# First stage of a two-layer latent/context kernel: one k-tile of modulation per pair of loads, and four products split in two parts

## The chip, the core and the metric

The kernel runs on one core of a Trainium2 chip. The metric is the device time of one execution in microseconds (us). Shorter is better. TensorE (PE) does the matmuls, VectorE (DVE), ScalarE (ACT) and GpSimd (POOL) the elementwise work. Data come by DMA: the queue of SyncE (SP, "q1" in the DMA views), that of ScalarE ("q10") and that of GpSimd ("q0"). All of them share the core's 16 DMA engines.

## The reference

Two layers work on 256 latent tokens of width 2048, and a context of 256 tokens is used by the first. Only the start of layer 0 is touched by the change:

```python
mod_lat = silu(c) @ ada_w[0] + ada_b[0]          # 2048 -> 6 * 2048: shift, scale, gate, ...
mod_ctx = silu(c_ctx) @ ada_w[0] + ada_b[0]
h_lat = rms_norm(x, g) * (1 + sc1) + sh1          # 256 x 2048
h_ctx = rms_norm(ctx, g) * (1 + csc1) + csh1      # 256 x 2048
qkv_lat, kv_ctx = h_lat @ w_qkv, h_ctx @ w_qkv[:, 2048:]
```

After it come attention, a dense MLP, the Fourier mixing layer, a second MLP and a norm. Everything is float32. A product of float32 matrices is made of three matmuls of a high and a low part: hi by hi, hi by lo, lo by hi.

## The kernel before

**Layout.** A k-tile is 128 of the 2048 input features. The tokens are turned so that features lie on the partitions (`xT`, then `h_hi` and `h_lo`, all in tile `hh`). The projection is done in groups of k-tiles: group 0 is k-tiles 0 and 1, group 1 is 2 and 3, then groups of four. Product `r` accumulates one block of 128 tokens by 512 output columns over the k-tiles of its group in one PSUM bank. Products 0 to 3 take w_qkv columns 0 to 1023 for the latent tokens. Each k-tile of these columns is one slice of the weights: slice 0 is k-tile 0, slice 1 is k-tile 1, each 128 x 1024. Two slices make one load of 1 MB.

**Weights.** SP loads `raw` (three buffers of 1 MB, `load_first` for loads 0 to 5, line 568). ACT copies a slice to its high part (`split_hi(s)`, line 727) and DVE subtracts to get the low part (`split_lo(s)`, line 1201). Before load 0 SP waits until modulation piece 1 has landed; then it issues raw load 0, raw load 1, the context (`c_rows`, 2 MB, line 594) and raw load 2 without another wait. Raw load 3 waits for slices 0 and 1 to be split, raw load 4 for slices 2 and 3, raw load 5 for slices 4 and 5.

**Modulation.** POOL loads `ada_w` in pieces of 1 MB (`load_start(n)`, line 652). Pieces 0 to 3 fill four `spare` buffers and are issued at once. Piece 4 waits for the context rows to land; pieces 4, 5, 6 are then issued together, and piece 7 waits for PE to have used piece 4, and so on. Pieces 0 to 7 (`first_v`) have rows of 256 columns, 1 KB, in DRAM: pieces 0 and 1 are the shift of k-tiles 0 and 1 (first and second half of the inputs), pieces 2 and 3 the scale of the same k-tiles. Pieces 4 to 7 do the same for k-tiles 2 and 3. Pieces from 8 on have rows of 512 columns, 2 KB.

PE multiplies a piece with `silu` (`first_piece(n)`, line 1887), into bank 6. When four pieces are in, ACT copies the rows out (`rows_out(0)`, line 777), PE turns them into columns (`first_cols(0)`, line 1896), and DVE adds the bias and makes the gain (`take_first`, lines 1318 and 1321). ACT then scales and shifts k-tiles 0 and 1 (`shape(0, 0)`, lines 789 and 793), and DVE makes the low part (`lower(0, 0)`, line 1351). Only then can product 0 start (lines 1848 to 1850).

**Order on each engine** is written out by hand. An engine does its instructions strictly in that order, waits included:

```python
# PE:  piece 0, piece 1, bias turns, piece 2, turn_input 0, 1, piece 3, turn_input 2, first_cols(0), turn_input 3, 4, 5,
#      product 0, 1, turn_input 6, 7, product 2, 3, ..., 8, piece 4, product 9, context turns, piece 5, product 10, ..., piece 6, ...
# ACT: x_out 0, 1, rows_out(0), split_hi(0), shape(0, 0), split_hi(1), x_out 2 to 5, split_hi(2), x_out 6, 7,
#      first_copy 0, 1, split_hi(3), first_copy 3, split_hi(4), split_hi(5), squares and norm of the context, ...
# DVE: take_first(0, 0), split_lo(0), lower(0, 0), split_lo(1), take_first(0, 1), split_lo(2), copy, split_lo(3), ...
```

`turn_input(i)` turns k-tiles 2i and 2i+1 of the normalised input into a PSUM bank (line 2116), and `x_out(i)` copies them to `xT` (line 769). Banks 0 to 3 hold turns 0 to 3 and are then the banks of products 0 to 3. The context rows are squared (line 755), normalised (line 1309) and turned (line 2146) later.

Of the kernel before, what the change touches and what calls it, by code (L numbers as in the profile page):

```python
# [136 lines left out]
def start_slot(n):  # L137

    return 3 + n if n < 4 else (n - 4) % 3


def vector_slot(i):

    if i < 8:
        return (7, 3)[i % 2]
    if 16 <= i < 48:
        return early_slot(i - 16)
    return i % 2
# [32 lines left out]

def start_count(n):

    return sum(start_slot(m) == start_slot(n) for m in range(n + 1))


def vector_count(i):

    return sum(start_slot(m) == vector_slot(i) for m in range(32)) + sum(vector_slot(m) == vector_slot(i) for m in range(i + 1))


def summed_before(i):
# [52 lines left out]
def layer_block(nc, x, c, ctx_in, c_ctx, ada_w, ada_b, norm_mix_g, norm_mlp_g, w_qkv, q_g, k_g, w_o,  # L245
# [118 lines left out]
    def sem(name):  # L364
        return stack.enter_context(nc.semaphore(name))
# [3 lines left out]
    c_in = sem("c_in")  # L369
    small_in = sem("small_in")  # L370
    x_in = sem("x_in")
    ctx_rows_in = sem("ctx_rows_in")
    rope_in_sem = sem("rope_in_sem")
    dft_in_sem = sem("dft_in_sem")
# [110 lines left out]
    wf_v = fourier_w[0].rearrange("(q k p) (b n) -> b q p k n", p=P, k=4, n=512)  # L485
    wqkv_first = w_qkv[0].rearrange("(g k p) (i n) -> g i p k n", p=P, k=2, n=NC)
    start_v = ada_w[0].rearrange("(q k p) (m g c) -> g m q p k c", p=P, k=4, g=4, c=512)
    first_v = ada_w[0].rearrange("(q k p) (m g c) -> g m q p k c", p=P, k=8, g=8, c=256)

    w1_v = [w1[l].rearrange("(q k p) (b n) -> b q p k n", p=P, k=4, n=512) for l in range(2)]  # L490

# [58 lines left out]
    def _(sp):  # L550
# [33 lines left out]
                                 gate_rows[v != 0][32 * j:32 * j + 32, :]).then_inc(gate_in, 16)  # L584

        sp.dma_start(ident[:, :], ident_in).then_inc(c_in, 16)
        sp.wait_ge(ada_in[start_slot(1)], 16)
        for p in range(24):
            if p < 6:
                load_first(p)  # L590
            else:
                load_columns(p, wqkv_v[p // 6, column_block(p)])
            if p == 1:
                sp.dma_start(c_rows[:, :, :], ctx_in[0].rearrange("(a p) d -> p a d", p=P)).then_inc(ctx_rows_in, 16)
            if p == 14:
                sp.wait_ge(prod_done, 48)
                sp.dma_start(rope[:, :, :, :], rope_in.rearrange("a (t p) d -> p a t d", p=P)).then_inc(rope_in_sem, 16)
                sp.dma_start(gains[:, 0, :], q_g[0].partition_broadcast(P)).then_inc(rope_in_sem, 16)
                sp.dma_start(gains[:, 1, :], k_g[0].partition_broadcast(P)).then_inc(rope_in_sem, 16)
# [41 lines left out]
    def _(pool):  # L641
        def load_start(n):

            if n >= 7:
                pool.wait_ge(ada_mm, n - 2)
            if n == 4:
                pool.wait_ge(ctx_rows_in, 16)
            if n < 8:
                dst, src = ring(start_slot(n)).rearrange("p (k c) -> p k c", k=8), first_v[n // 4, n % 4 // 2, n % 2]
            else:  # L650
                dst, src = ring(start_slot(n)).rearrange("p (k c) -> p k c", k=4), start_v[n // 8, n % 8 // 4, n % 4]
            pool.dma_start(dst, src).then_inc(ada_in[start_slot(n)], 16)

        def load_vector(i):

# [55 lines left out]
    def _(act):  # L711
# [60 lines left out]
        def rows_out(c):  # L772
# [60 lines left out]
        def heads_out(i, bank):  # L833
# [7 lines left out]
                dst = qT[:, 4 * b:4 * b + 4, tt * P:(tt + 1) * P]  # L841
            act.activation(dst, src, ACT.Copy).then_inc(head_T_out, 1)

        x_out(0)
        x_out(1)
        rows_out(0)
        split_hi(0)
        shape(0, 0)
        split_hi(1)
        x_out(2)  # L850
        x_out(3)
        x_out(4)
        x_out(5)
        split_hi(2)
# [341 lines left out]
    def _(dve):  # L1196
# [115 lines left out]
        def take_first(c, n):  # L1312

            dst, kts = (mod_col, modc_col)[n], group_tiles(c)
            dve.wait_ge(col_mm, c + 1)
            dve.wait_ge(vec_ready, 3)
            cols = ps[:, 6, 0:8].rearrange("p (m t v) -> p v m t", m=2, v=2)
            nc.vector.tensor_tensor(dst[:, 0:32].rearrange("p (m k) -> p m k", m=2)[:, :, kts], cols[:, n],
                                    bias_col[:, 0:32].rearrange("p (m k) -> p m k", m=2)[:, :, kts], ALU.add).then_inc(start_mods, 1)
            dve.wait_ge(start_mods, 2 * c + n + 1)  # L1320
            nc.vector.scalar_tensor_tensor(a_col[:, n, kts], dst[:, 16 + kts.start:16 + kts.stop], 1.0,
                                           misc[:, V_MIX + kts.start:V_MIX + kts.stop], ALU.add, ALU.mult).then_inc(a_ready, 1)

        def copy_first(r):

# [20 lines left out]
        def lower(c, n):  # L1346

            src, hi, lo = ((xT, h_hi, h_lo), (ctxT, hc_hi, hc_lo))[n]
            kts = group_tiles(c)
            dve.wait_ge(hhi_ready, 2 * c + n + 1)  # L1350
            nc.vector.tensor_tensor(lo[:, kts, :], src[:, kts, :], hi[:, kts, :].bitcast(F32),  # L1351
                                    ALU.subtract).then_inc(h_ready, 1)

        def add_product(r):

# [71 lines left out]
        for i, (dst, w) in enumerate(((bias_col[:, 0:96], 96), (bias_col[:, 96:192], 96), (misc[:, 32:96], 64))):  # L1427
            dve.wait_ge(vec_T, 3)
            nc.vector.tensor_copy(dst, ps[:, 7, i * P:i * P + w]).then_inc(vec_ready, 1)
        take_first(0, 0)  # L1430
        split_lo(0)
        lower(0, 0)
        split_lo(1)
        take_first(0, 1)
        split_lo(2)
        copy_first(2)
# [406 lines left out]
    def _(pe):  # L1843
# [8 lines left out]
        def tile_out(bank0, j):  # L1852
            return ps[:, bank0 + j // 2, (j % 2) * T:(j % 2 + 1) * T]

        def product(r):

            p, cb, tt = product_at(r)
            c = r // 16
            if r < 5:
                pe.wait_ge(x_T_out, (1, 2, 3, 4, 7)[r])  # L1860
            elif r == 33:
                pe.wait_ge(ctx_T_out, 7)
            else:
                pe.wait_ge(*flushed(bank_before(r)))
            hi, lo = (h_hi, h_lo) if tt < 2 else (hc_hi, hc_lo)
            pe.wait_ge(h_ready, 2 * c + 1 + tt // 2)
            tok = slice((tt % 2) * P, (tt % 2 + 1) * P)
            kts = group_tiles(c)
            n = kts.stop - kts.start
            for k in range(n):  # L1870
                sl, b = (2 * p + k // 2, k % 2) if n == 4 else (2 * p + k, cb % 2)
                w = slice(512 * b, 512 * (b + 1))
                pe.wait_ge(lo_ready, sl + 1)
                ins = three(ps[:, product_bank(r), :], hi[:, kts.start + k, tok], lo[:, kts.start + k, tok], w_hi[:, sl % SPLIT, w],
                            w_lo[:, sl % SPLIT, w], k == 0, k == n - 1)
            ins.then_inc(prod_done, 1)

        def first_piece(n):

            slot, m, q = start_slot(n), n % 4 // 2, n % 2  # L1880
            pe.wait_ge(ada_in[slot], 16 * start_count(n))
            if n == 4:
                pe.wait_ge(start_mods, 2)
            w = ring(slot).rearrange("p (k c) -> p k c", k=8)
            for k in range(8):
                j = 32 * (k % 4)
                ins = mm(ps[j:j + 32, 6, m * T:(m + 1) * T], silu[:, 8 * q + k, :], w[:, k, :], start=(q == 0 and k < 4),
                         stop=(q == 1 and k >= 4), skip_group_check=True)
            ins.then_inc(ada_mm, 1)

        def first_cols(c):

            pe.wait_ge(rows_copied, c + 1)
            pe.wait_ge(pick_ready, 2)
            for f in range(4):
                ins = mm(ps[:, 6, 2 * f:2 * f + 2], ada_rows[:, f * P:(f + 1) * P], pick_first[:, :], start=True, stop=True)
            ins.then_inc(col_mm, 1)

        def ada_piece(n):

# [221 lines left out]
        pe.wait_ge(small_in, 64)  # L2122
        for i, n in enumerate((96, 96, 64)):
            nc.tensor.transpose(ps[:, 7, i * P:i * P + n], vec_rows[0:n, i, :], ident[0:n, 0:n]).then_inc(vec_T, 1)
        first_piece(2)
        turn_input(0)
        turn_input(1)
        first_piece(3)
        turn_input(2)
        first_cols(0)  # L2130
        for i in range(3, 6):
            turn_input(i)

        def turn_ctx(i):

# [319 lines left out]
```

## Time and profile before

| | |
|---|---|
| three timed executions | 2003.6, 2004.11, 2005.1 us (median 2004.11) |
| profiled execution, own time | 2005.52 us |
| its span, first to last instruction | 2003.6 us |
| mean granted TensorE clock | 0.996 of 2.4 GHz |
| PE busy | 1965.9 us, 98% of the span |
| DVE busy, ACT busy | 1391.5 us, 969.3 us |
| moved by DMA | 542.80 MB |

A profile view gives times from the start of the span. In a row of the timeline the first number is the start, the second how long, then engine, line, operation, tile written from tile read, size, and how many such instructions; in brackets stands how long the engine had been idle and what ended the idle time.

### The profile page before, as it was taken

The page shows a single profiled execution, that of the slowest core. Times are in us where ns is not written, and L with a number is a line of the kernel's source. Part 1 is how long each engine was busy: PE and PEld are TensorE (multiplying, and loading weights), DVE is VectorE, ACT ScalarE, POOL GpSimd, SP SyncE. Part 2 cuts the span into 40 slices and gives each one's busy share as a digit, 9 for nine tenths or more (in the row PEclk, how much of TensorE's full clock was granted, in tenths as well). Part 3 has the DMA queues.
Part 4 walks back from the last instruction along what each step waited for, and adds up shares of the span by engine and source line. Part 5 has one row for each costly group of instructions (what it writes and reads, how often), then busy time and mean ns, then how long its engine had stood idle before and what let it go on. Part 6 is the DMA issues. An engine that isn't in the chain of part 4 may idle for free.

```text
span 2003.6 us, 24992 instructions
## 1 busy us (share of the span) xinstructions
PE 1965.9 (98%) x10188; PEld 1609.5 (80%) x10188; DVE 1391.5 (69%) x1424; ACT 969.3 (48%) x1265; POOL 110.9 (6%) x196
## 2 busy tenths in 40 slices
PE   6999989999999999999999999999999999999998
PEld 4677756778888888888888888788888888888886
DVE  3666998889867787788888675766666455555556
ACT  6432565455544455544444464555554454444444
POOL 1111001000000000000000000000000000000000
PEclk9999999999999999999999999999999999999999
DMA  9998768779989899799999626577776566555653
GB/s 359 338 378 319 277 257 297 272 252 323 353 293 348 313 360 364 262 367 363 355 395 383 219 85 193 175 252 253 257 251 220 187 192 210 189 192 198 218 190 126
DMA packets 152261, 542.80 MB, mean 271 GB/s; under 512 B 9393, under 2 KB 10577, under 8 KB 114641
## 3 DMA queue, kind: packets, MB, share of 16 engines
q1 hardware_dynamic: 119312, 335.77, 47.9%
q0 software_dynamic: 31744, 201.34, 27.1%
q10 hardware_dynamic: 1090, 4.09, 0.5%
q8 instruction: 81, 1.33, 0.3%
q14 instruction: 34, 0.28, 0.0%
HBM read 535.91 MB, written 2.10 MB: 269 GB/s over the span
## 4 chain that ended last, share of the span: by engine, by line
PE 94%; DVE 3%; ACT 1%; DMA 1%; issue 1%; POOL 0%; ACTq 0%; DVEq 0%; POOLq 0%
PE ps L2098 13%; PE ps L2036 12%; PE ps L2032 12%; PE ps L2035 11%; PE ps L2096 11%; PE ps L2099 6%; PE ps L1848 6%; PE ps L2095 6%; PE ps L1849 5%; PE ps L1850 5%; PE ps L2257 1%; PE ps L1913 1%; PE ps L2204 1%; DMA spare<-in_ada_w 1%; PE ps L2242 1%
## 5 line engine op out<-in xcount | busy, mean ns | idle before, releaser
L1201 DVE TENSOR_TENSOR w_lo<-raw,w_hi 128x1024 fp32r<-128x1024 f32 x616 | 749.5, 1223 | 467.9 <-ACT w_hi L727 467.6
L727 ACT ACTIVATE w_hi<-raw 128x1024 fp32r<-128x1024 f32 x616 | 649.4, 1059 | 845.7 <-PE ps L2036 345.8
L2098 PE MATMUL ps<-hh,w_hi 128*128 128x512 f32 x1088 | 427.5, 398 | 1.1 <-DVE hh L1627 1.1
L2032 PE MATMUL ps<-w_hi,hh 128*128 128x512 f32 x992 | 385.9, 389 | 0.0
L2036 PE MATMUL ps<-w_hi,hh 128*128 128x512 f32 x992 | 385.9, 389 | 0.0
L2035 PE MATMUL ps<-w_lo,hh 128*128 128x512 f32 x992 | 385.9, 389 | 0.0
L2096 PE MATMUL ps<-hh,w_hi 128*128 128x512 f32 x960 | 379.9, 396 | 0.0
L2099 PE MATMUL ps<-hh,w_lo 128*128 128x256 f32 x1088 | 302.9, 278 | 0.0
L2095 PE MATMUL ps<-hh,w_lo 128*128 128x256 f32 x960 | 267.5, 279 | 0.0
L2099 PEld LDWEIGHTS ps<-hh,w_lo 128*128 128x128 f32 x1088 | 205.7, 189 | 40.9
L2035 PEld LDWEIGHTS ps<-w_lo,hh 128*128 128x128 f32 x992 | 186.2, 188 | 38.9
L2032 PEld LDWEIGHTS ps<-w_hi,hh 128*128 128x128 f32 x992 | 186.2, 188 | 38.5
L2036 PEld LDWEIGHTS ps<-w_hi,hh 128*128 128x128 f32 x992 | 186.2, 188 | 38.4
L2098 PEld LDWEIGHTS ps<-hh,w_hi 128*128 128x128 f32 x1088 | 207.2, 190 | 11.2 <-issue 5.0
L2095 PEld LDWEIGHTS ps<-hh,w_lo 128*128 128x128 f32 x960 | 180.2, 188 | 43.7
L1229 DVE SCALAR_TENSOR_TENSOR ada_sum<-ada_raw,silu,ada_sum 128x2048 f32<-128x2048 f32 x83 | 194.7, 2346 | 2.7 <-DMA ada_raw<-in_ada_w 2.6
L1848 PE MATMUL ps<-w_hi,hh 128*128 128x512 f32 x448 | 190.8, 426 | 3.5 <-DVE hh L1351 1.6
L2096 PEld LDWEIGHTS ps<-hh,w_hi 128*128 128x128 f32 x960 | 179.9, 187 | 0.0
L1849 PE MATMUL ps<-w_lo,hh 128*128 128x512 f32 x448 | 175.8, 392 | 0.0
L1850 PE MATMUL ps<-w_hi,hh 128*128 128x512 f32 x448 | 175.2, 391 | 0.0
L693 POOL DMA_DIRECT2D ada_raw<-in_ada_w x132 | 70.5, 534 | 1138.3 <-DVE ada_sum L1229 584.3
L1848 PEld LDWEIGHTS ps<-w_hi,hh 128*128 128x128 f32 x448 | 84.5, 189 | 39.7 <-issue 14.4
(252 smaller groups left out, 1620.4 us busy)
## 6 DMA issues: line engine op xcount, KB each, us to landing
raw<-in_mlp_w SPq DMA_DIRECT2D x256, 1024.0 KB, 5.3
ada_raw<-in_ada_w POOLq DMA_DIRECT2D x151, 1024.0 KB, 6.2
spare<-in_ada_w POOLq DMA_DIRECT2D x29, 1024.0 KB, 6.6
raw<-in_attn_w_qkv SPq DMA_DIRECT2D x24, 1024.0 KB, 10.1
raw<-in_attn_w_o SPq DMA_DIRECT2D x16, 1024.0 KB, 5.7
raw<-in_fourier_w_o SPq DMA_DIRECT2D x16, 1024.0 KB, 5.1
g_row<-in_ada_w POOLq DMA_DIRECT2D x12, 1024.0 KB, 9.0
g_row<-gate_rows SPq DMA_DIRECT2D x48, 64.0 KB, 5.2
```

The costliest lines, as they stand in the source:

```text
L727: act.activation(w_slot(s)[0], raw[:, piece % RAW, s % 2, :], ACT.Copy).then_inc(hi_ready, 1)
L1201: nc.vector.tensor_tensor(lo, raw[:, s // 2 % RAW, s % 2, :], hi.bitcast(F32), ALU.subtract).then_inc(lo_ready, 1)
L1848: mm(dst, w_h, m_h, start=start, stop=False, skip_group_check=True)
L1849: mm(dst, w_h, m_l, start=False, stop=False, skip_group_check=True)
L1850: return mm(dst, w_l, m_h, start=False, stop=stop, skip_group_check=True)
L2032: ins = mm(bank_of(tt, nb), h_hi[:, k % KT, tok], hi[:, cols], start=start, stop=False)
L2035: mm(bank_of(tt, nb), h_hi[:, k % KT, tok], lo[:, cols], start=False, stop=False)
L2036: return mm(bank_of(tt, nb), h_lo[:, k % KT, tok], hi[:, cols], start=False, stop=stop)
L2095: mm(ps[:, bank, 0:T], w_lo[:, s % SPLIT, w], h_hi[:, k, :], start=False, stop=False, skip_group_check=True)
L2096: ins = mm(both, w_hi[:, s % SPLIT, w], hh[:, k, :, :], start=False, stop=(k == KT - 1), skip_group_check=True)
L2098: mm(both, w_hi[:, s % SPLIT, w], hh[:, k, :, :], start=(k == 0), stop=False, skip_group_check=True)
L2099: ins = mm(ps[:, bank, 0:T], w_lo[:, s % SPLIT, w], h_hi[:, k, :], start=False, stop=(k == KT - 1), skip_group_check=True)
```

## The change

1. **Modulation pieces 0 to 7.** A piece now holds shift and scale of one k-tile, 128 columns each, instead of 256 columns of one of them. It is loaded by two DMAs of 512 KB, with rows of 512 bytes in DRAM. Pieces 0 and 1 are k-tile 0, pieces 2 and 3 are k-tile 1; pieces 4 to 7 likewise for k-tiles 2 and 3. Each piece counts 32 on its semaphore.
2. **SP's waits.** Raw load 0 still waits for piece 1. Raw load 1, and with it the context and raw load 2 behind it, now wait for piece 3.
3. **PE.** Pieces 0 and 1 go to bank 6, pieces 2 and 3 to bank 5. The columns of k-tile 0 (`first_cols(0, (0, 1))`) come before piece 2; those of k-tile 1 after turn 3. Products 0 to 3 are begun with k-tile 0 alone (12 matmuls), then comes turn 4, and then the four products are completed with k-tile 1, turn 5 behind the first, turns 6 and 7 behind the second.
4. **ACT.** New order: rows of k-tile 0, x_out 0, shape k-tile 0, split_hi(0), rows of k-tile 1, x_out 1, split_hi(1), x_out 2, 3, shape k-tile 1, x_out 4, 5, split_hi(2), then as before.
5. **DVE.** Columns of k-tile 0, low part of k-tile 0, split_lo(0), columns of k-tile 1, split_lo(1), low part of k-tile 1, then the context's columns and split_lo(2) as before.

The rest of the kernel is the same.

```diff
-    first_v = ada_w[0].rearrange("(q k p) (m g c) -> g m q p k c", p=P, k=8, g=8, c=256)
+    first_v = ada_w[0].rearrange("(q k p) (m g t c) -> g t q p k m c", p=P, k=8, g=8, t=2, c=P)
...
-        sp.wait_ge(ada_in[start_slot(1)], 16)
         for p in range(24):
+            if p < 2:
+                sp.wait_ge(ada_in[start_slot(1 + 2 * p)], 32)
...
             if n < 8:
-                dst, src = ring(start_slot(n)).rearrange("p (k c) -> p k c", k=8), first_v[n // 4, n % 4 // 2, n % 2]
+                rows, src = ring(start_slot(n)).rearrange("p (k m c) -> p k m c", k=8, m=2), first_v[n // 4, n % 4 // 2, n % 2]
+                for m in range(2):
+                    pool.dma_start(rows[:, :, m, :], src[:, :, m, :]).then_inc(ada_in[start_slot(n)], 16)
...
+        def first_rows(kt):
+
+            act.wait_ge(ada_mm, 2 * kt + 2)
+            act.activation(ada_rows[:, kt * T:(kt + 1) * T], ps[:, 6 - kt, kt * T:(kt + 1) * T],
+                           ACT.Copy).then_inc((early_rows, rows_copied)[kt], 1)
...
+        def shape_first(kt):
+
+            act.wait_ge((a_first, a_ready)[kt], 1)
+            act.wait_ge(x_T_out, 1)
+            act.activation(xT[:, kt, :], xT[:, kt, :], ACT.Identity, bias=mod_col[:, kt:kt + 1],
+                           scale=a_col[:, 0, kt:kt + 1]).then_inc(mod_done, 1)
+            shaped[0] += 1
+            act.wait_ge(mod_done, shaped[0])
+            act.activation(h_hi[:, kt, :], xT[:, kt, :], ACT.Copy).then_inc((first_hi, hhi_ready)[kt], 1)
...
+        first_rows(0)
         x_out(0)
+        shape_first(0)
+        split_hi(0)
+        first_rows(1)
         x_out(1)
-        rows_out(0)
-        split_hi(0)
-        shape(0, 0)
         split_hi(1)
         x_out(2)
         x_out(3)
+        shape_first(1)
         x_out(4)
...
-        take_first(0, 0)
+        take_first_k(0)
+        lower_first(0)
         split_lo(0)
-        lower(0, 0)
+        take_first_k(1)
         split_lo(1)
+        lower_first(1)
...
+        first_cols(0, (0, 1))
         first_piece(2)
         turn_input(0)
         turn_input(1)
         first_piece(3)
         turn_input(2)
-        first_cols(0)
-        for i in range(3, 6):
-            turn_input(i)
+        turn_input(3)
+        first_cols(0, (2, 3))
...
+        for r in range(4):
+            product(r, 0)
+        turn_input(4)
         for r in range(77):
-            product(r)
+            product(r, 1 if r < 4 else None)
+            if r == 0:
+                pe.wait_ge(start_mods, 2)
+                turn_input(5)
```

## Rows read from the trace of the kernel before

**Rows 1.** The page: the chain that ended last, share of the span by engine.

```profile
PE 94%; DVE 3%; ACT 1%; DMA 1%; issue 1%; POOL 0%; ACTq 0%; DVEq 0%; POOLq 0%
```

**Rows 2.** Busy time by stretch: stretch, us, busy of each engine, clock, DMA share, GB/s.

```profile
31.00:35.00 4.00, 4.00 (x14) 3.17 (x14) 1.23 (x1) 1.29 (x2) 2.63 (x3) 0.60 1.02 409
...
40.00:50.00 10.00, 9.84 (x64) 7.11 (x66) 7.36 (x13) 8.69 (x23) 0.88 (x1) 1.00 1.02 375
...
60.00:100.00 40.00, 39.97 (x268) 27.43 (x267) 24.24 (x40) 18.36 (x28) 7.13 (x11) 1.00 0.93 342
100.00:250.00 150.00, 149.99 (x857) 110.73 (x856) 112.19 (x137) 57.96 (x113) 18.52 (x30) 1.00 0.88 325
```

**Rows 3.** Timeline, modulation pieces 1 to 3 on PE, SP's loads, first product.

```profile
15.81 0.90 SPq L568 DMA_DIRECT2D raw<-in_attn_w_qkv  x2
15.84 1.94 PE L1887 MATMUL ps<-spare,silu 128*32 128x256 f32 x16 [1.26 <-DMA spare<-in_ada_w]
...
18.85 1.93 PE L1887 MATMUL ps<-spare,silu 128*32 128x256 f32 x16 [0.27 <-DMA spare<-in_ada_w]
...
22.97 1.52 PE L1887 MATMUL ps<-spare,silu 128*32 128x256 f32 x16 [0.28 <-DMA spare<-in_ada_w]
...
29.29 0.47 PE L1848 MATMUL ps<-w_hi,hh 128*128 128x512 f32 x1 [1.65 <-DVE hh L1351]
```

**Rows 4.** Timeline, POOL's wait for the context, slice 3, pieces 4 and 6.

```profile
32.17 1.75 POOL L652 DMA_DIRECT2D ada_raw<-in_ada_w  x2 [27.22 <-DMA c_rows<-in_ctx]
...
37.03 1.08 ACT L727 ACTIVATE w_hi<-raw 128x1024 fp32r<-128x1024 f32 x1
...
39.43 0.50 PE L1848 MATMUL ps<-w_hi,hh 128*128 128x512 f32 x1 [0.47 <-DVE w_lo L1201]
...
45.78 1.07 PE L1887 MATMUL ps<-ada_raw,silu 128*32 128x256 f32 x16
48.61 1.09 PE L2146 MATMUL ps<-ident,c_rows 128*128 128x128 f32 x8 [0.16 <-DVE c_rows L1309]
...
53.09 1.07 PE L1887 MATMUL ps<-g_row,silu 128*32 128x256 f32 x16
```

**Rows 5.** The chain that ended last, parts between 31 and 48 us.

```profile
31.49 0.43 PE ps L1849
...
36.66 0.23 PE ps L1850
...
40.80 2.46 ACT sq_in L755 x8
```

**Rows 6.** DMA by queue, 15.8 to 18.5 us (1 KB rows): packets, MB, share of 16 engines.

```profile
q0 software_dynamic: 246, 0.94, 103.1%
```

**Rows 7.** DMA by queue, 23.5 to 25.5 us: raw loads, 4 KB rows.

```profile
q1 hardware_dynamic: 208, 0.82, 102.4%
```

**Rows 8.** DMA by queue, 57 to 59 us: modulation pieces with 2 KB rows.

```profile
q0 software_dynamic: 196, 0.78, 99.7%
```

**Rows 9.** DMA by queue, 44.5 to 47 us: both queues at work.

```profile
q1 hardware_dynamic: 141, 0.58, 59.4%
q0 software_dynamic: 101, 0.36, 42.3%
```

**Rows 10.** Groups by line, 0 to 50 us: count, busy, mean ns.

```profile
L727 ACT ACTIVATE w_hi<-raw 128x1024 fp32r<-128x1024 f32 x7 | 7.3, 1057 | 0.0
...
L769 ACT ACTIVATE xT<-ps 128x512 f32<-128x512 f32 x8 | 4.3, 594 | 6.4 <-PE ps L2116 6.4
...
L789 ACT ACTIVATE xT<-xT,mod_col,a_col 128x256 f32<-128x256 f32 x2 | 1.1, 594 | 0.6 <-DVE a_col L1321 0.6
```

More of the change, by code:

```diff
@@ L182, in start_count @@
 def start_count(n):
-    return sum(start_slot(m) == start_slot(n) for m in range(n + 1))
+    return sum((1 + (m < 8)) * (start_slot(m) == start_slot(n)) for m in range(n + 1))
 def vector_count(i):
-    return sum(start_slot(m) == vector_slot(i) for m in range(32)) + sum(vector_slot(m) == vector_slot(i) for m in range(i + 1))
+    return sum((1 + (m < 8)) * (start_slot(m) == vector_slot(i)) for m in range(32)) + sum(vector_slot(m) == vector_slot(i) for m in range(i + 1))
 def summed_before(i):
@@ L371, in layer_block @@
     x_in = sem("x_in")
+    first_hi = sem("first_hi")
+    first_h = sem("first_h")
+    first_mods = sem("first_mods")
+    a_first = sem("a_first")
+    col_first = sem("col_first")
+    early_rows = sem("early_rows")
     ctx_rows_in = sem("ctx_rows_in")
@@ L648, in load_start @@
             if n < 8:
-                dst, src = ring(start_slot(n)).rearrange("p (k c) -> p k c", k=8), first_v[n // 4, n % 4 // 2, n % 2]
+                rows, src = ring(start_slot(n)).rearrange("p (k m c) -> p k m c", k=8, m=2), first_v[n // 4, n % 4 // 2, n % 2]
+                for m in range(2):
+                    pool.dma_start(rows[:, :, m, :], src[:, :, m, :]).then_inc(ada_in[start_slot(n)], 16)
             else:
                 dst, src = ring(start_slot(n)).rearrange("p (k c) -> p k c", k=4), start_v[n // 8, n % 8 // 4, n % 4]
-            pool.dma_start(dst, src).then_inc(ada_in[start_slot(n)], 16)
+                pool.dma_start(dst, src).then_inc(ada_in[start_slot(n)], 16)
         def load_vector(i):
@@ L1316, in take_first @@
             dve.wait_ge(vec_ready, 3)
-            cols = ps[:, 6, 0:8].rearrange("p (m t v) -> p v m t", m=2, v=2)
-            nc.vector.tensor_tensor(dst[:, 0:32].rearrange("p (m k) -> p m k", m=2)[:, :, kts], cols[:, n],
-                                    bias_col[:, 0:32].rearrange("p (m k) -> p m k", m=2)[:, :, kts], ALU.add).then_inc(start_mods, 1)
+            for t, kt in enumerate(range(kts.start, kts.stop)):
+                at = slice(kt, 17 + kt, 16)
+                nc.vector.tensor_tensor(dst[:, at], ps[:, 6 - (kt == 1), 4 * t + n:4 * t + 4:2], bias_col[:, at],
+                                        ALU.add).then_inc((first_mods, start_mods)[t], 1)
+            dve.wait_ge(first_mods, 2 * c + n + 1)
             dve.wait_ge(start_mods, 2 * c + n + 1)
@@ L1322, in take_first, with take_first_k @@
                                            misc[:, V_MIX + kts.start:V_MIX + kts.stop], ALU.add, ALU.mult).then_inc(a_ready, 1)
+        def take_first_k(kt):
+            dve.wait_ge((col_first, col_mm)[kt], 1)
+            if kt == 0:
+                dve.wait_ge(vec_ready, 3)
+            at = slice(kt, 17 + kt, 16)
+            nc.vector.tensor_tensor(mod_col[:, at], ps[:, 6 - kt, 4 * kt:4 * kt + 4:2], bias_col[:, at],
+                                    ALU.add).then_inc((first_mods, start_mods)[kt], 1)
+            dve.wait_ge((first_mods, start_mods)[kt], 1)
+            nc.vector.scalar_tensor_tensor(a_col[:, 0, kt:kt + 1], mod_col[:, 16 + kt:17 + kt], 1.0,
+                                           misc[:, V_MIX + kt:V_MIX + kt + 1], ALU.add, ALU.mult).then_inc((a_first, a_ready)[kt], 1)
         def copy_first(r):
@@ L1352, in lower, with lower_first @@
                                     ALU.subtract).then_inc(h_ready, 1)
+        def lower_first(kt):
+            dve.wait_ge((first_hi, hhi_ready)[kt], 1)
+            nc.vector.tensor_tensor(h_lo[:, kt, :], xT[:, kt, :], h_hi[:, kt, :].bitcast(F32),
+                                    ALU.subtract).then_inc((first_h, h_ready)[kt], 1)
         def add_product(r):
@@ L1853, in tile_out, with product @@
             return ps[:, bank0 + j // 2, (j % 2) * T:(j % 2 + 1) * T]
-        def product(r):
+        def product(r, part=None):
             p, cb, tt = product_at(r)
             c = r // 16
-            if r < 5:
+            if part == 1:
+                pass
+            elif r < 5:
                 pe.wait_ge(x_T_out, (1, 2, 3, 4, 7)[r])
@@ L1865, in product @@
             hi, lo = (h_hi, h_lo) if tt < 2 else (hc_hi, hc_lo)
-            pe.wait_ge(h_ready, 2 * c + 1 + tt // 2)
+            if part == 0:
+                pe.wait_ge(first_h, 1)
+            else:
+                pe.wait_ge(h_ready, 2 * c + 1 + tt // 2)
             tok = slice((tt % 2) * P, (tt % 2 + 1) * P)
@@ L1869, in product @@
             n = kts.stop - kts.start
-            for k in range(n):
+            for k in range(n) if part is None else (part,):
                 sl, b = (2 * p + k // 2, k % 2) if n == 4 else (2 * p + k, cb % 2)
@@ L1875, in product @@
                             w_lo[:, sl % SPLIT, w], k == 0, k == n - 1)
-            ins.then_inc(prod_done, 1)
+            if part != 0:
+                ins.then_inc(prod_done, 1)
         def first_piece(n):
-            slot, m, q = start_slot(n), n % 4 // 2, n % 2
+            slot, t, q = start_slot(n), n % 4 // 2, n % 2
             pe.wait_ge(ada_in[slot], 16 * start_count(n))
@@ L1886, in first_piece, with first_cols @@
                 j = 32 * (k % 4)
-                ins = mm(ps[j:j + 32, 6, m * T:(m + 1) * T], silu[:, 8 * q + k, :], w[:, k, :], start=(q == 0 and k < 4),
+                ins = mm(ps[j:j + 32, 6 - (n // 2 == 1), t * T:(t + 1) * T], silu[:, 8 * q + k, :], w[:, k, :], start=(q == 0 and k < 4),
                          stop=(q == 1 and k >= 4), skip_group_check=True)
             ins.then_inc(ada_mm, 1)
[L1891 to L1897, printed above, removed]
+        def first_cols(c, part=(0, 1, 2, 3)):
+            if part == (0, 1):
+                pe.wait_ge(early_rows, 1)
+                pe.wait_ge(pick_ready, 2)
+            else:
+                pe.wait_ge(rows_copied, c + 1)
+            for f in part:
+                ins = mm(ps[:, 6 - (c == 0 and f > 1), 2 * f:2 * f + 2], ada_rows[:, f * P:(f + 1) * P], pick_first[:, :], start=True,
+                         stop=True)
+            ins.then_inc(col_first if part == (0, 1) else col_mm, 1)
         def ada_piece(n):
```

## The prediction

> **What bounds the kernel now.** I read the page first: PE makes 94% of the chain that ended last [rows 1]. Then the busy time by stretch: from 60 to 250 us PE stands still for 0.04 us in all [rows 2]. So the first stage is worth one number: how much earlier or later PE comes out of it, at about 60 us. A shift there is kept, because nothing behind it waits for something that isn't itself shifted.
>
> Next I read the timeline of the first stage and its DMA. The reader is to see two things. PE waits for pieces 1, 2 and 3 one after the other, at 15.84, 18.85 and 22.97 us, and product 0 starts at 29.29 us after 1.65 us of idling [rows 3]. And the DMA engines have no free time: their share is 1.02 from 31 to 35 us and still from 40 to 50 us [rows 2]. In this stage a byte that comes later makes everything behind it later. The slack between a landing and its use is short, so both sides have to be worked out.
>
> **The price of the 512-byte rows.** No row of before shows such rows on POOL's queue, so I bound them by longer rows. Time of one load of 1 MB (1.049e6 bytes) on all 16 engines is share x stretch / MB x 1.049. With 4 KB rows: 1.024 x 2.0 / 0.82 x 1.049 = 2.62 us [rows 7]. With 2 KB rows: 0.997 x 2.0 / 0.78 x 1.049 = 2.68 us [rows 8]. With 1 KB rows: 1.031 x 2.7 / 0.94 x 1.049 = 3.10 us [rows 6]. From 4 KB to 1 KB there are three more rows in each 4 KB, for 0.48 us, 0.16 us each. From 1 KB to 512 bytes there are four more: 0.64 us, 3.74 us for one piece. That is the value I take. The low end is no extra at all; the high end is twice my value, 1.3 us, since the steps grow: 0.06 us from 4 KB to 2 KB, 0.42 from 2 KB to 1 KB.
>
> The Trainium skill speaks against this term: DMA: Bandwidth & Descriptors, Specifications, gives 512 bytes as the smallest transfer at line rate. By it pieces of 512-byte rows would cost no more than before. The trace agrees only in part, since 1 KB rows, which the rule calls full rate too, take 3.10 us against 2.62 us for 4 KB rows [rows 6, 7].
>
> **The change part by part.**
>
> *Pieces 0 to 3.* Four pieces, 4 x 0.64 = +2.6 us, on a queue that PE waits for each time. Piece 1 is usable at 15.84 + 1.3 = 17.1, piece 2 at 18.85 + 1.9 = 20.8, piece 3 at 22.97 + 2.6 = 25.6 us [rows 3]. x shares the queue's time with the first of them, which adds 0.3: 25.9 us. The additional issues (one is 1.75 / 2 = 0.88 us [rows 4], eight in all, 7 us) are over long before.
>
> *SP's waits.* Raw load 0 is issued at 17.1 instead of 15.81 us [rows 3]; it still shares with piece 3, and is in at about 27 us. Raw load 1 used to be issued at once behind it. Now it is issued at 25.9 us, when nothing else is queued. Between SP's issue and the first bytes no row gives a time with idle engines. I take 1 us between nothing and 4 (rival 4), so the engines stand still for about 0.9 us. The context lies behind raw load 1. It releases POOL at 32.17 us now [rows 4]; after, at 32.17 + 2.6 + 0.9 = 35.7 us.
>
> *ACT, DVE and PE up to slice 3.* The columns of k-tile 0 are ready early, hidden by the wait for piece 2. Turns 0 and 1 follow piece 2 until 24.7 us, x_out 0 and the shaping of k-tile 0 are done at 25.3 us. Then ACT stands at split_hi(0), which needs raw load 0 at 27 us, and the rows of k-tile 1 are queued behind it. From there, with 1.06 us for a split, 0.59 for x_out and 0.59 for a shaping of 256 [rows 10], and about 0.35 for half-size copies: split_hi(0) 27.1 to 28.2, rows 28.5, x_out 1 29.1, split_hi(1) 30.2, x_out 2 and 3 31.2, shaping of k-tile 1 32.2, low part 32.6. PE does the 12 begun matmuls in 29.4 to 32.1 (split_lo(0) is done at 29.4), turn 4 to 32.6, product 0 is completed at 33.3, product 1 at 34.5, turn 7 at 35.5, product 3 at 36.9. ACT in the same time: x_out 5 at 34.3, split_hi(2) 35.4, x_out 6 and 7 36.5, first_copy 0 and 1 37.6. So split_hi(3) starts at 37.6 against 37.03 us now, and the wait of PE for slice 3 ends at 40.0 against 39.43 us [rows 4]. The four products are ready early, and what they gain is lost in ACT's queue. Of the gain, nothing is left; +0.5 us.
>
> *Context norm.* It comes behind split_hi(5) on ACT: its squares start at 40.80 + 0.5 us [rows 5], well after the context's 35.7. Its turns are at 48.61 + 0.5 us on PE [rows 4]. No new wait.
>
> *Pieces 4, 5, 6.* They are issued when the context is in, 35.7 us. From there until piece 6 is in, the engines have to move raw loads 2 and 3 (5.2 us), pieces 4, 5, 6 (3 x 3.74 = 11.2) and raw loads 4 and 5 (5.2). Those last two are tied to the slices, not to the context, so they aren't shifted and now fall into the same time; two busy queues share the engines about evenly (59.4% and 42.3% [rows 9]), which lets them through. Sum: 35.7 + 21.6 = 57.3 us. PE wants piece 6 at 53.09 + 0.5 us and doesn't wait for it now [rows 4]. So PE comes 57.3 - 53.1 = **4.2 us** later out of piece 6. Piece 4 (about 44.5 us) is in time for 45.78, piece 5 (about 51) takes some 1.5 us of the same 4.2. Pieces 7 and on are issued when PE has used an earlier one, so they shift with it.
>
> *Clock.* Before, PE's idling around 27 to 31 us was followed by a stretch at half the clock: 0.60 granted in 31 to 35 us, a matmul 0.43 us in place of 0.23 [rows 2, 5], some 12 matmuls, at most 2 us. The new idling before pieces 5 and 6 is longer, about 4 us. I take that it brings one such stretch and that half of it falls on the wait: +1.0 us.
>
> *Sum.* 4.2 + 1.0 = +5.2 us. The profiled execution, 2005.52 us (span 2003.6 and 1.9 around it), would be 2010.7. It stands 1.4 above the median of the runs, 2004.11. Predicted median: 2004.11 + 5.2 = **2009.3 us**.
>
> **Rivals.**
>
> 1. *Short rows cost nothing* (what the skill's rule gives). Then piece 3 is usable at 23.3 (turned columns are 0.4 in front of it), raw load 0 at 24.6, split_lo(0) done at 26.9, and by the same ACT sums split_hi(3) starts at 35.0: 2.0 us before 37.03. The context is in at 33, piece 6 is in at about 51, wanted at 51.1. Result 2004.11 - 2.0 = 2002.1 us. It decides at 0.1 us for a piece and below. Against it: 3.10 against 2.62 us [rows 6, 7].
> 2. *The rows cost, but raw loads 4 and 5 don't overtake piece 6.* Then one or both (2.6 to 5.2 us) leave the sum, and piece 6 is in at 52 to 54.7, so the loss is 0.5 to 2 us from ACT's queue and this wait, without a clock stretch: 2005 to 2006.5 us. For it: from 44.5 to 47 us neither queue is clearly first.
> 3. *The whole head start is kept.* Product 3 is done earlier by the full 1.4 us of its second half and by the earlier start, and no landing is in the way: some 4 us, 2000 us. That asks that ACT isn't behind at split_hi(3), whereas two x_out, two copies and a split lie there in a row.
> 4. *The empty DMA time is longer.* If SP's issue at 25.9 us takes as long to the first bytes as raw load 0's does now (issued 15.81, the engines still full of pieces at 18.5 us [rows 3, 6]), some 3 us more, then everything up to piece 6 shifts on: +7.5 to +8.5, 2012 us.
>
> **How the numbers follow.** The forecast (+3.5 to +6.5) has 0.45, rival 1 0.12, rival 2 0.22, rival 3 0.06, rival 4 0.15. About 0.2%, 4 us, is what a measurement tells from no change. Faster by more than that is rival 3 and little else: 0.06. Within it lie rivals 1 and 2 and the lower end of the forecast, 0.06 of it: 0.40. Slower: 0.54. The range leaves out rival 3 and the far end of rival 4: 2001.5 to 2012. The likeliest case alone is 2007.6 to 2010.6.
>
> **What the profile after would show.** Piece 3 on PE at about 26 us, not 23; a modulation-only stretch below 300 GB/s; a dip of the DMA share near 27 us; POOL's wait for the context ending near 36 us; split_hi(3) within 1 us of 37; a wait of PE for DMA before pieces 5 and 6, the second ending near 57 us; a lower clock soon after. If piece 3 is at 23 us, my price is wrong. If piece 6 is waited for by nobody although piece 3 is late, the queue sum is.

## The result: 0.26% slower, as forecast

Timed against the kernel before, the changed kernel takes 1.0026 of its time, interval 1.0017 to 1.0036. The medians are 2010.78 us (7 executions) and 2005.1 us (7). The forecast was 2009.3 us from a base of 2004.11, +5.2; measured is +5.7, and by the ratio +5.2. The profiled execution spans 2009.0 us against 2003.6.

The chain that ended last of the changed kernel, first 58 us (start, how long, what), shows the place:

```profile
1.26 6.30 POOL spare L658 x7
7.56 17.78 DMA spare<-in_ada_w
...
25.35 0.37 SPq L574
...
25.77 10.84 DMA c_rows<-in_ctx
...
36.89 3.51 POOL ada_raw L658 x4
...
41.26 16.43 DMA g_row<-in_ada_w
...
57.74 1.07 PE ps L1942 x16
```

Up to 57.74 us nothing that computes is in it. Modulation pieces 0 to 3 come in, SP issues the next loads, the context comes in, POOL issues pieces 4 to 6, and piece 6 releases PE at 57.74 us.

The timeline of the changed kernel, the rows that answer to [rows 3, 4] (line numbers have moved: 1942 is the product with a modulation piece, 574 the raw loads, 658 the short pieces, 736 split_hi):

```profile
16.92 1.93 PE L1942 MATMUL ps<-spare,silu 128*32 128x256 f32 x16 [1.65 <-DMA spare<-in_ada_w]
...
25.38 1.94 PE L1942 MATMUL ps<-spare,silu 128*32 128x256 f32 x16 [1.00 <-DMA spare<-in_ada_w]
...
37.34 1.09 ACT L736 ACTIVATE w_hi<-raw 128x1024 fp32r<-128x1024 f32 x1
...
39.74 0.51 PE L1897 MATMUL ps<-w_hi,hh 128*128 128x512 f32 x1 [1.87 <-DVE w_lo L1228]
46.09 1.07 PE L1942 MATMUL ps<-ada_raw,silu 128*32 128x256 f32 x16
48.92 1.09 PE L2205 MATMUL ps<-ident,c_rows 128*128 128x128 f32 x8 [0.16 <-DVE c_rows L1336]
52.21 1.28 PE L1942 MATMUL ps<-ada_raw,silu 128*32 128x256 f32 x16 [2.20 <-DMA ada_raw<-in_ada_w]
...
54.02 0.63 PE L1898 MATMUL ps<-w_lo,hh 128*128 128x512 f32 x1
...
57.74 1.07 PE L1942 MATMUL ps<-g_row,silu 128*32 128x256 f32 x16 [0.45 <-DMA g_row<-in_ada_w]
```

Up to the context's turns PE is only 0.3 us behind before (48.92 against 48.61). The 4.65 us (57.74 against 53.09) come between 49 and 58 us: 2.65 in two waits for loads, and most of the rest in a stretch at half the clock between them, which shortened the second wait. Then they stay. SP's first store of the output, before and after:

```profile
1989.14 11.09 SPq L626 DMA_DIRECT2D out<-y_rows  x8
```

```profile
1994.51 11.09 SPq L633 DMA_DIRECT2D out<-y_rows  x8
```

That is 5.4 us, 4.65 of them there since piece 6. Busy time by stretch of the changed kernel, to be set against [rows 2]:

```profile
25.00:31.00 6.00, 5.62 (x35) 4.12 (x36) 3.04 (x5) 4.65 (x9) 0.00 (x0) 1.00 0.92 338
31.00:35.00 4.00, 4.00 (x26) 3.37 (x25) 0.79 (x5) 1.91 (x4) 0.00 (x0) 1.00 0.99 414
...
40.00:50.00 10.00, 9.84 (x57) 7.06 (x56) 7.16 (x12) 9.10 (x24) 4.00 (x5) 1.00 1.00 321
50.00:60.00 10.00, 7.36 (x53) 4.83 (x52) 2.92 (x5) 1.72 (x3) 1.51 (x2) 0.83 1.03 331
```

The reader is to see three things. From 40 to 50 us the DMA engines are as busy as before and move 321 GB/s in place of 375. From 25 to 31 us their share is below 1. And the half clock has moved: the stretch from 31 to 35 us now has 1.00, and it is 50 to 60 us that has 0.83. So the 0.3 us above compare a stretch at full clock with one that had 0.60 before; against the kernel before without such a stretch (the run with two DMAs below) the changed kernel is 2.4 us late at the same turns, 48.92 against 46.55. DMA by queue from 15.8 to 18.5 us, as [rows 6]:

```profile
q0 software_dynamic: 223, 0.78, 102.8%
```

1.028 x 2.7 / 0.78 x 1.049 = 3.73 us for one piece (0.78 is rounded, which leaves 0.02 us open). The forecast was 3.74.

### The profile page after: what moved, and what is told of

The parts are those of the page before. It is cut to its first block, busy times and chain, and to the rows that moved or that the text cites. A ratio compares the mean times of both kernels' runs of the same rounds, so it can differ in the third digit from the quotient of the medians.

```text
span 2009.0 us, 25017 instructions
## 1 busy us (share of the span) xinstructions
PE 1967.6 (98%) x10188; PEld 1610.2 (80%) x10188; DVE 1391.9 (69%) x1430; ACT 970.1 (48%) x1267; POOL 118.4 (6%) x204
## 4 chain that ended last, share of the span: by engine, by line
PE 92%; DVE 3%; DMA 3%; ACT 1%; issue 1%; POOL 1%; ACTq 0%; SPq 0%; DVEq 0%; POOLq 0%
PE ps L2157 13%; PE ps L2091 11%; PE ps L2094 11%; PE ps L2095 11%; PE ps L2155 11%; PE ps L2158 6%; PE ps L1897 6%; PE ps L2154 6%; PE ps L1898 5%; PE ps L1899 5%; PE ps L2322 1%; PE ps L1972 1%; PE ps L2269 1%; DMA spare<-in_ada_w 1%; DMA g_row<-in_ada_w 1%; PE ps L2307 1%
## 6 DMA issues: line engine op xcount, KB each, us to landing
raw<-in_attn_w_qkv SPq DMA_DIRECT2D x24, 1024.0 KB, 11.2
```

## The experiments

A single profiled execution wanders by about 2 us between 60 us and its end (partly by where stretches at half the clock fall): with short rows alone PE is 2.9 us late at piece 6 and 5.1 at the first store of the output. So the mechanism is read from the start of piece 6 on PE, and the size of the loss from the timed ratio. Diffs show the edited loads and waits; three dots stand for lines left out, among them the counts on the semaphores.

### Row length or number of DMAs: two runs on the kernel before

Only the loads of pieces 0 to 7 are edited, first with 512-byte rows:

```diff
...
-            pool.dma_start(dst, src).then_inc(ada_in[start_slot(n)], 16)
+                for m in range(2):
+                    pool.dma_start(dst[:, :, P * m:P * (m + 1)], src[:, :, P * m:P * (m + 1)]).then_inc(ada_in[start_slot(n)], 16)
```

> The kernel before, unchanged but for one thing: each of modulation pieces 0 to 7 is loaded by two DMAs with 512-byte rows, as after the change, into the same places. No split products, SP's waits as before. Theory (row length costs 0.64 us a piece while the DMA engines are full): piece 3 on PE at 22.97 + 2.6 = 25.5 us, POOL's wait for the context ends at 34.8 us, piece 6 on PE at 34.8 + 21.6 = 56.4 us against 53.09, so +3.3 us. Rival A (the hand-written order of ACT and PE is what costs): nothing but the order could cost, so 0 us and piece 6 at 53.1. Rival B (it is the number of DMAs, not their rows): also about +3.3; the next run tells these apart.

Then with two DMAs of 1 KB rows:

```diff
...
+                    pool.dma_start(dst[:, 4 * m:4 * m + 4, :], src[:, 4 * m:4 * m + 4, :]).then_inc(ada_in[start_slot(n)], 16)
```

> The kernel before with two DMAs for each of pieces 0 to 7, but the rows stay 1 KB long (each DMA takes half of the k-tiles). Theory (row length): piece 3 within 0.3 us of 22.97, piece 6 at 53.1, time within 0.5 us of before. Rival B (number of DMAs, their issues and semaphores): as the run with 512-byte rows, +3.3 us, piece 3 at 25.5 us.

Measured: 1.0018 (1.0009 to 1.0028) with short rows and 0.9995 (0.9985 to 1.0004) with two DMAs of long rows. The timeline with short rows, POOL, ACT (slice 3 split) and PE:

```profile
34.49 3.50 POOL L651 DMA_DIRECT2D ada_raw<-in_ada_w  x4 [26.06 <-DMA c_rows<-in_ctx]
```

```profile
37.46 1.08 ACT L729 ACTIVATE w_hi<-raw 128x1024 fp32r<-128x1024 f32 x1
```

```profile
25.44 1.07 PE L1889 MATMUL ps<-spare,silu 128*32 128x256 f32 x16 [1.22 <-DMA spare<-in_ada_w]
...
56.03 1.07 PE L1889 MATMUL ps<-g_row,silu 128*32 128x256 f32 x16 [2.44 <-DMA g_row<-in_ada_w]
```

and with two DMAs of 1 KB rows, ACT and PE:

```profile
35.08 1.08 ACT L729 ACTIVATE w_hi<-raw 128x1024 fp32r<-128x1024 f32 x1
```

```profile
23.05 1.07 PE L1889 MATMUL ps<-spare,silu 128*32 128x256 f32 x16 [0.83 <-DMA spare<-in_ada_w]
...
37.47 0.50 PE L1850 MATMUL ps<-w_hi,hh 128*128 128x512 f32 x1 [0.50 <-DVE w_lo L1203]
...
52.19 1.07 PE L1889 MATMUL ps<-g_row,silu 128*32 128x256 f32 x16 [1.08 <-DMA g_row<-in_ada_w]
```

Expected for short rows were 25.5, 34.8, 56.4 and +3.3 us; found 25.44, 34.49, 56.03 and +3.6 by the ratio. The rows alone, with no other edit, bring two thirds of the loss. The number of DMAs brings nothing; rival B falls. The second trace says more: here the early stretch was at full clock (1.00 granted from 31 to 35 us, against 0.60 in [rows 2]), PE was 2 us early at slice 3 (37.47 against 39.43), and it was 0.9 us early at piece 6, after a wait. So in the kernel before, too, the loads in front of piece 6 are close behind PE: most of a head start ends there.

### The changed kernel with the long rows back

All orders of the change and SP's two waits, pieces 0 to 7 by one DMA with 1 KB rows. Its modulation is not the reference's; the loads and the shapes of the instructions are the ones wanted:

```diff
-    first_v = ada_w[0].rearrange("(q k p) (m g t c) -> g t q p k m c", p=P, k=8, g=8, t=2, c=P)
+    first_v = ada_w[0].rearrange("(q k p) (m g c) -> g m q p k c", p=P, k=8, g=8, c=256)
...
+                dst, src = ring(start_slot(n)).rearrange("p (k c) -> p k c", k=8), first_v[n // 4, n % 4 // 2, n % 2]
-                for m in range(2):
-                    pool.dma_start(rows[:, :, m, :], src[:, :, m, :]).then_inc(ada_in[start_slot(n)], 16)
```

> The changed kernel with all of its orders and SP's two waits, but pieces 0 to 7 are loaded by one DMA with 1 KB rows each, as before the change. The pieces then hold other columns than the code takes them for, so the modulation of k-tiles 0 to 3 is not the reference's. Theory: piece 3 on PE at 23.3 us or a little before, split_hi(3) at 35.0 in place of 37.34, piece 6 at about 51, so 2.0 us faster than before the change. Rival A (the order costs): piece 6 at 57.7 still, +4.7 us.

```profile
34.85 1.09 ACT L734 ACTIVATE w_hi<-raw 128x1024 fp32r<-128x1024 f32 x1
```

```profile
37.25 0.50 PE L1895 MATMUL ps<-w_hi,hh 128*128 128x512 f32 x1 [1.86 <-DVE w_lo L1226]
...
48.43 1.07 PE L1940 MATMUL ps<-ada_raw,silu 128*32 128x256 f32 x16 [0.91 <-DMA ada_raw<-in_ada_w]
53.50 1.07 PE L1940 MATMUL ps<-g_row,silu 128*32 128x256 f32 x16 [1.54 <-DMA g_row<-in_ada_w]
```

Measured 1.0006 (0.9996 to 1.0015): no difference. The early part went as expected (split_hi(3) at 34.85 us, expected 35.0). The expected gain of 2.0 us did not come: piece 6 was in at 53.5 us, not at 51. Rival A falls as well, since PE is 4.2 us earlier at piece 6 than in the changed kernel; but my own figure for this case was wrong.

And the gain of 2.0 us was not one of the order to begin with. This trace has the full clock from 31 to 35 us, the one before had 0.60. The kernel before at full clock (the run with two DMAs) splits slice 3 at 35.08 us and starts its product at 37.47, against 34.85 and 37.25 here: 0.2 us. With short rows the pair is 37.46 (short rows alone) and 37.34 (the changed kernel), both at full clock: 0.1 us. What the expectations below call the head start of the split products, 2.2 us, is therefore nearly all the stretch at half the clock in the trace before.

Two more runs went after that. Their edits: SP's second wait out, and then also

```diff
+            if p == 4:
+                sp.wait_ge(ada_in[start_slot(6)], 16)
```

> The changed kernel's orders on PE, ACT and DVE with the loads as before the change in everything: 1 KB rows, one DMA a piece, and SP without the second wait. As in the other run with 1 KB rows, the modulation of k-tiles 0 to 3 is not the reference's. What is open: with 1 KB rows PE was 2.2 us early at slice 3 (37.25 against 39.43 us), and still 0.4 us late at piece 6. Theory (the engines' full queue in front of piece 6 takes the head start): without SP's wait the context is in 1 us earlier than 33.26, piece 6 at 52.5 in place of 53.50 and still waited for by PE, so -0.6 us against before. Rival (SP's wait alone took it): PE doesn't wait for piece 6 and reaches it at 50.9, -2.2 us.

> The same, and raw load 4 waits on SP until piece 6 has landed. Theory: the queue in front of piece 6 is 5.2 us shorter, PE doesn't wait for it and is there at 50.9 us, -2.2 us against before: the whole head start of the split products is then to be seen, and perhaps half of it is lost again before pieces 7 to 12. Rival (something else than loads holds PE between slice 3 and piece 6): no earlier than 52.5.

Without SP's second wait:

```profile
51.73 1.07 PE L1940 MATMUL ps<-g_row,silu 128*32 128x256 f32 x16 [0.93 <-DMA g_row<-in_ada_w]
```

and with raw load 4 behind piece 6:

```profile
45.30 1.07 PE L1942 MATMUL ps<-ada_raw,silu 128*32 128x256 f32 x16
...
52.26 1.07 PE L1942 MATMUL ps<-g_row,silu 128*32 128x256 f32 x16
...
58.63 1.07 PE L1942 MATMUL ps<-ada_raw,silu 128*32 128x256 f32 x16 [1.18 <-DMA ada_raw<-in_ada_w]
```

Measured 1.0001 (0.9992 to 1.0011) and 1.0000 (0.9991 to 1.0009). The context was not in 1 us earlier than 33.26, as expected, but at 33.27; piece 6 came 0.8 us earlier than the 52.5 expected. Without the wait PE is still held by piece 6, at 51.73: 1.4 us earlier than before the change, only 0.5 more than the 0.9 of the run with two DMAs, where no product was split. With piece 6 let through, PE doesn't wait for it, and waits 1.18 us for piece 7 instead, starting it at 58.63 against 58.22 us before the change. It was not at 50.9 for piece 6 either: piece 4 started at 45.30 in place of 43.77, behind a stretch at half the clock (0.80 granted in 35 to 40 us and 0.93 in 40 to 50) that followed PE's wait for slice 3. So even with loads that cost no more than before, the split products bring nothing that can be measured. Against the kernel before at full clock, piece 7 starts at 56.88 us without SP's second wait and at 58.63 with raw load 4 behind piece 6, against 57.32.

### The queue in front of piece 6

The changed kernel, raw load 4 issued when piece 6 is in:

```diff
+            if p == 4:
+                sp.wait_ge(ada_in[start_slot(6)], 32)
```

> The changed kernel, where SP also waits until piece 6 has landed before it issues raw load 4 (and raw load 5 behind it). Theory (raw loads 4 and 5, 5.2 us of all engines, take their half of the time in front of piece 6): piece 6 is in at 57.7 - 5.2 = 52.5 us and PE doesn't wait for it, PE reaches it at 53.4, so +0.3 to +0.8 us against before in place of +4.7. Rival C (piece 6 is late only because the context and so its issue are late): piece 6 at 57 us still, +4 us.

```profile
53.18 1.07 PE L1944 MATMUL ps<-g_row,silu 128*32 128x256 f32 x16
...
70.04 1.07 PE L1974 MATMUL ps<-ada_raw,silu 128*32 128x256 f32 x16 [1.32 <-DMA ada_raw<-in_ada_w]
74.86 0.42 PE L1974 MATMUL ps<-ada_raw,silu 128*32 128x256 f32 x4 [0.80 <-DMA ada_raw<-in_ada_w]
```

Measured 1.0014 (1.0005 to 1.0024). At piece 6 it went as expected: 53.18 us, no wait. Rival C falls: the context lets POOL go at 35.68 us, 3.5 us later than before the change, and that alone doesn't hold PE; the queue does. But +0.3 to +0.8 us was wrong for the whole. The 5.2 us of raw loads 4 and 5 now lie in front of pieces 7 and on, and PE waits for pieces 10 and 11, 2.1 us together (the view ends at 75 us and shows a part of piece 11). The debt is moved and only half is forgiven.

### SP's wait, and the short rows that serve nothing

SP's second wait taken back in the changed kernel:

```diff
-            if p < 2:
-                sp.wait_ge(ada_in[start_slot(1 + 2 * p)], 32)
+            if p == 0:
+                sp.wait_ge(ada_in[start_slot(1)], 32)
```

> The changed kernel with SP's second wait taken back: raw load 1, the context and raw load 2 are issued right behind raw load 0, after piece 1. Theory (the wait leaves the engines empty for about 0.9 us near 27 us, and nothing else comes of it): DMA share from 25 to 31 us back from 0.92 to 1.02, piece 3 still at 25.4 us, the context about 0.9 us earlier than 36.89, piece 6 at 56.8 in place of 57.74, +3.8 us against before. Rival (the wait shields piece 3): piece 3 later than 25.4 by 1 us or more, piece 6 no earlier, +4.7 us.

Busy time by stretch, then the timeline:

```profile
25.00:31.00 6.00, 5.37 (x34) 3.88 (x35) 2.88 (x5) 4.64 (x9) 0.00 (x0) 1.00 1.03 418
```

```profile
25.63 1.93 PE L1942 MATMUL ps<-spare,silu 128*32 128x256 f32 x16 [0.99 <-DMA spare<-in_ada_w]
...
56.13 1.71 PE L1942 MATMUL ps<-g_row,silu 128*32 128x256 f32 x16 [2.83 <-DMA g_row<-in_ada_w]
```

The wait shields nothing: piece 3 is at 25.63 without it and at 25.38 with it, the same difference that piece 1 has already (17.19 and 16.92). It costs the empty engines: the share is back at 1.03, POOL is released at 34.69 in place of 36.89 us, 2.2 us earlier (0.9 expected), and piece 6 is 1.6 us earlier (0.9 expected). The empty time accounts for about 0.6 us of that. For a part of the rest spread is enough: in the three runs that keep SP's wait and the short rows of pieces 0 to 3, POOL is released at 35.62, 35.68 and 36.08 us. In the time nothing of that is seen, 1.0026 (1.0015 to 1.0037). In the profiled execution the 2.83 us wait was followed by a half clock, in which piece 6 itself took 1.71 us in place of 1.07.

Pieces 4 to 7 with 1 KB rows and one DMA, the rest as changed:

```diff
+    second_v = ada_w[0].rearrange("(q k p) (m g c) -> g m q p k c", p=P, k=8, g=8, c=256)
...
-            if n < 8:
+            if n < 4:
...
+            elif n < 8:
+                dst, src = ring(start_slot(n)).rearrange("p (k c) -> p k c", k=8), second_v[1, n % 4 // 2, n % 2]
```

> The changed kernel, but pieces 4 to 7 are loaded by one DMA each with 1 KB rows, as before the change (no product of k-tiles 2 and 3 is split, so their short rows serve nothing). Theory (0.64 us for each short piece in front of piece 6): piece 6 at 57.74 - 3 x 0.64 = 55.8 us, +2.8 us against before. Rival (only pieces 0 to 3 matter, since those are the ones PE waits for): 57.7 still, +4.7 us.

```profile
47.86 1.07 PE L1947 MATMUL ps<-ada_raw,silu 128*32 128x256 f32 x16
52.03 1.07 PE L1947 MATMUL ps<-ada_raw,silu 128*32 128x256 f32 x16 [0.61 <-DMA ada_raw<-in_ada_w]
56.65 1.07 PE L1947 MATMUL ps<-g_row,silu 128*32 128x256 f32 x16 [1.08 <-DMA g_row<-in_ada_w]
```

Measured 1.0020 (1.0011 to 1.0030). Piece 6 is 1.1 us earlier, 1.9 were expected. Of the 1.1 us 0.8 are the context, which released POOL at 36.08 in place of 36.89 us; from there to piece 6 it took 20.57 in place of 20.85 us. In that time the engines moved 3.80 MB for SP's queue, against 3.25 MB in the changed kernel: at 2.62 us for 1 MB that is 1.4 us, most of what the longer rows save. The sign is as expected, but one execution doesn't tell this saving from the spread of the context.

Both at once, and the same edit of SP on the kernel before:

> Both at once: pieces 4 to 7 with 1 KB rows, and raw load 4 waits on SP until piece 6 has landed. Theory: no wait of PE for pieces 5 and 6 (piece 6 in at about 51, PE there at 53.2), and the debt that the run with the wait alone paid later (2.35 us before pieces 10 and 11) shrinks by the 4 x 0.64 us saved to nothing, so PE leaves this stage within 0.5 us of before; time within 1 us of before. Rival (the debt is that of pieces 0 to 3 and of the empty engines, and is paid anyway): a wait of 1 to 2 us before pieces 8 to 12.

> The kernel before the change with SP's wait for piece 6 in front of raw load 4 as its only edit. In the run with two DMAs a piece, PE came 1.08 us early to piece 6 and waited. Theory (the DMA queue in front of piece 6 bounds this stage before the change too): piece 6 is not waited for, and where the early stretch isn't at half the clock PE reaches it at about 51.2 in place of 52.2 to 53.1; 0.5 to 1.5 us faster than before, too little for the interval. Rival (raw loads 4 and 5 are wanted by then): a wait for slice 8 or for later pieces gives it back, 0 to +2 us.

The first:

```profile
54.38 1.07 PE L1949 MATMUL ps<-g_row,silu 128*32 128x256 f32 x16
...
74.56 0.64 PE L1979 MATMUL ps<-ada_raw,silu 128*32 128x256 f32 x8 [0.66 <-DMA ada_raw<-in_ada_w]
```

the second:

```profile
53.47 1.07 PE L1889 MATMUL ps<-g_row,silu 128*32 128x256 f32 x16
```

The first measured 1.0015 (1.0005 to 1.0024), not within 1 us of before as expected: PE waits for nothing at piece 6 but is 1.3 us late there, behind a stretch at half the clock (0.66 granted in 40 to 45 us), and 0.66 us are paid at piece 11 (again only its part before 75 us is shown). The rival asked for 1 to 2 us. (The 2.35 us that the expectation gives for the run with the wait alone are the 2.1 us above.) The second measured 1.0001 (0.9992 to 1.0010). In its profiled execution the early stretch was at half the clock (0.57 in 31 to 35 us), PE was late enough not to have waited anyway, and the expected gain of 0.5 to 1.5 us can't be told. No version tried is measurably faster than the kernel before.

## Why the prediction was right

**The row price.** 0.64 us for a piece was a straight line through two of the three row lengths of [rows 6, 7, 8], 4 KB and 1 KB, drawn on by a factor of two. Measured 0.63 (3.73 against 3.10). So close a hit is partly luck: the 2 KB rows lie 0.10 us below that line, the 4 KB rows are SP's queue and the others POOL's, and POOL's queue alone (2.68 to 3.10 for two more rows in each 4 KB) would have given 0.84. By the measured price, the rule that 512 bytes are enough for line rate (the Trainium skill, DMA: Bandwidth & Descriptors, Specifications) doesn't hold here: on POOL's queue rows of 512 bytes, 1 KB and 2 KB take 3.73, 3.10 and 2.68 us for 1 MB. The run with short rows alone shows this to be the cause of two thirds of the loss.

**The parts at piece 6.** Short rows alone bring PE there at 56.03 us, the changed orders with them at 56.13 (SP's wait undone), SP's wait on top at 57.74. So the 4.65 us are 2.9 for the rows, 0.1 for the orders and 1.6 for the wait, each from single executions, and the wait's share doesn't show in the timed ratio. The prediction gave the orders 0.5 and the wait 0.9. Against the kernel before at full clock (52.19 us) the whole is 5.55 us and the rows 3.84 of it; the other two stay.

**Landings.** Forecast and found: piece 1 17.1 and 16.92, piece 3 25.9 and 25.38, slice 3's wait 40.0 and 39.74, context turns 49.1 and 48.92, piece 6 57.3 and 57.74. The context was forecast to release POOL at 35.7; it was 36.89 here and 35.68 in the run with raw load 4 held back, whose start is the same. I hadn't allowed for that spread.

**The head start lost in ACT's queue.** The time is right: split_hi(3) at 37.6 forecast, 37.34 found. The words are only half right. ACT was not just behind with its work: it stood still for PE's turns 4 and 5, which the new order of PE puts behind the begun products.

```profile
32.86 0.60 ACT L778 ACTIVATE xT<-ps 128x512 f32<-128x512 f32 x1 [1.56 <-PE ps L2175]
33.99 0.60 ACT L778 ACTIVATE xT<-ps 128x512 f32<-128x512 f32 x1 [0.53 <-PE ps L2175]
```

From 33.99 us on ACT's queue sets the pace, and PE then waits 1.87 us for slice 3, against 0.47 before. I also compared with 37.03 and 39.43 us of a trace that had half the clock just ahead of them; at full clock the kernel before is at 35.08 and 37.47. Which of the two most timed executions have isn't known.

**The queue sum.** 21.6 us from the context to piece 6 forecast; found 57.74 - 36.89 = 20.9. DMA by queue in that time:

```profile
q0 software_dynamic: 1026, 3.76, 59.9%
q1 hardware_dynamic: 856, 3.25, 41.4%
```

The total is better than its halves. POOL's queue took 12.5 us of all engines (forecast 11.2; it had moved 0.6 MB more than the three pieces) and SP's 8.6 (forecast 10.4). And it offset the late context: 1.2 us late there, 0.7 us less here. That raw loads 4 and 5 take a share in it was half of the argument. With them held back PE is at piece 6 4.6 us earlier (53.18 against 57.74) and doesn't wait; the context's earlier landing in that run accounts for at most 1.2 of that. Rival 2 is out.

**The clock.** This term was mis-sized. I took +1.0 us; at piece 6 it cost nothing that shows. The half clock came (0.83 in 50 to 60 us), but between pieces 5 and 6, where the products at 0.63 us only shortened the next wait for the same load, down to 0.45. In return the 5.4 us at the end are 0.7 more than the 4.65 of piece 6. Of these, 0.6 come between 1967 and 1986 us: ACT waits 1.46 us for a late load of the MLP weights (0.59 before) and PE 0.32 us for its low part. Short rows alone don't have that wait (ACT 0.48 us), so nothing ties it to the change. The sum of 5.2 is thus better than its parts, and that is luck: 4.2 should have been 4.65, and no run shows the 1.0.

**Rival 1** was wrong in steps of its own. "Piece 6 is in at about 51" was not: 53.50 with SP's wait and 51.73 without. The forecast's own queue sum with 3.10 us for a piece would have given 33.0 + 5.2 + 9.3 + 5.2 = 52.7 us. And its 2.0 us at slice 3 were counted from the trace at half the clock. **Rival 3**'s 4 us were never there: at the same clock and rows the split products start slice 3 0.1 to 0.2 us sooner. **Rival 4** asked for an empty time of 4 us; the share of 0.92 over 6 us is 0.5 to 0.7 us.

## What to carry to other kernels

When the DMA engines are full for the whole stage, find the last wanted load first, and count everything that the engines must move in front of it, the loads of other queues too. Most of a head start in the compute ends there: of 2 us at slice 3, 0.9 were left at piece 6 in the run with two DMAs. Before crediting a new order with a head start, compare two executions that had the same clock in that stretch: here 2.2 us shrank to 0.2. An order that starts products earlier also delays what stands behind them, here the turns that ACT needed.

Then price a finer layout by row length. The time for the same bytes at longer rows gave a price that held for a factor of two beyond them, but the points were not on one line; it is an estimate with a range. Letting one load pass another moves such a debt: of 4.6 us at piece 6, 2.1 came back before pieces 10 and 11.

## What the runs showed of the hardware

- The cost of a modulation load is in its rows, not in the number of DMAs: twice as many DMAs with 1 KB rows measured 0.9995, twice as many with 512-byte rows 1.0018.
- Two queues with work share the engines about evenly by time, also when one of them has 512-byte rows. DMA by queue of the changed kernel, 44.5 to 47 us:

```profile
q0 software_dynamic: 118, 0.42, 54.1%
q1 hardware_dynamic: 108, 0.44, 47.8%
```

- A stretch at half the clock (matmuls of 0.63 us in place of 0.39) came behind PE's idling in seven of the twelve profiled executions between 20 and 100 us, in different places: 31 to 35 us before the change, 50 to 60 after it, 38 to 42 in the run with long rows and raw load 4 held back. The same idling doesn't always bring it: PE waited 1.86 to 1.87 us for slice 3 in eight executions, and it followed there in three. Whether it costs anything depends on whether a wait for a load follows that would have been there anyway: none of it showed in the changed kernel, and 2.0 us at slice 3 in the kernel before (39.43 against 37.47).
